# Three conditioning blocks of the second layer computed by VectorE and GpSimd beside the first layer's output product

## What is computed

```python
def adaln(cond, w, b):
    m = jax.nn.silu(cond) @ w + b
    return jnp.split(m[:, None, :], 6, axis=-1)      # shift, scale, gate, and again

for l in range(2):
    mp, ms = adaln(c_ctx[None, :], ada_w[l], ada_b[l]), adaln(c, ada_w[l], ada_b[l])
    hp, hs = modulate(xp, norm_mix[l], mp[0], mp[1]), modulate(xs, norm_mix[l], ms[0], ms[1])
    # layer 0: windowed attention and pooling, then @ a_w_out; layer 1: Fourier mixing, @ f_w_out
    xp, xs = xp + mp[2] * op, xs + ms[2] * os_
    # then a mixture of experts of the same kind, modulated with mp[3..5] and ms[3..5]
```

## Time and profile before

| | us |
|---|---|
| median of 3 runs (772.98 to 773.32) | 773.24 |
| the profiled execution | 773.66 |
| its span, first to last instruction | 771.9 |
| TensorE busy | 754.7 |
| VectorE busy | 373.5 |
| ScalarE busy | 172.9 |
| GpSimd busy | 2.4 |

### The profile page before, as it was taken

How to read it: one execution, slowest core, us unless ns; L and a number is a source line. 1 busy time by engine, 2 the same in 40 slices (tenths; PEclk the granted TensorE clock), 3 DMA queues, 4 the chain that set the end, 5 groups by cost and what they waited for, 6 DMA issues and landing times.

```text
span 771.9 us, 9987 instructions
## 1 busy us (share of the span) xinstructions
PE 754.7 (98%) x3907; PEld 372.4 (48%) x3907; DVE 373.5 (48%) x826; ACT 172.9 (22%) x431; POOL 2.4 (0%) x12
## 2 busy tenths in 40 slices
PE   8999999999999999999998999999999999999997
PEld 3364546445535444434345658445545345444434
DVE  2216174137635345336327996636733454345316
ACT  4111565026301110110115203016211101110111
POOL 0000000000000000000000000000000000000000
PEclk9999999999999999999999999999999999999999
DMA  8979999228999999999999967056699999999994
GB/s 340 427 222 429 428 427 427 110 108 313 349 391 425 427 429 426 428 428 426 422 413 428 425 286 324 3 218 240 250 375 425 428 426 429 425 430 424 424 416 183
DMA packets 32850, 277.04 MB, mean 359 GB/s; under 512 B 7789, under 2 KB 8833, under 8 KB 12833
## 3 DMA queue, kind: packets, MB, share of 16 engines
q1 hardware_dynamic: 32305, 274.96, 86.4%
q10 hardware_dynamic: 432, 1.28, 0.5%
q0 software_dynamic: 64, 0.13, 0.0%
HBM read 274.65 MB, written 1.70 MB: 358 GB/s over the span
## 4 chain that ended last, share of the span: by engine, by line
PE 87%; DMA 4%; DVE 4%; ACT 2%; issue 1%; DVEq 1%; SPq 0%; ACTq 0%
PE bank L2130 28%; PE bank L2155 14%; PE bank L1996 11%; PE bank L2109 5%; PE bank L2161 5%; PE bank L2555 5%; PE bank L2425 4%; PE bank L1924 3%; DMA ring<-in_moe_w 3%; PE bank L2386 3%; DMA ring<-in_ada_w 1%; PE bank L2498 1%; PE bank L2477 1%; PE bank L2141 1%; PE bank L2136 1%
## 5 line engine op out<-in xcount | busy, mean ns | idle before, releaser
L2130 PE MATMUL bank<-ring,Z 128*64 128x512 f32 x1024 | 226.5, 594 | 0.5 <-DMA ring<-in_moe_w 0.5
L2130 PEld LDWEIGHTS bank<-ring,Z 128*64 128x64 f32 x1024 | 72.6, 137 | 137.2 <-issue 135.2
L2155 PE MATMUL bank<-ring,Z 128*64 128x512 f32 (+1 forms) x544 | 113.9, 570 | 0.2 <-DMA ring<-in_moe_w 0.2
L1996 PE MATMUL bank<-ring,T 128*128 128x512 f32 x192 | 83.6, 593 | 0.4 <-issue 0.4
L2155 PEld LDWEIGHTS bank<-ring,Z 128*64 128x64 f32 x544 | 37.9, 137 | 68.2 <-issue 66.1
L1609 DVE TENSOR_TENSOR Z<-Z,bank 128x512 f32<-128x512 f32 x16 | 11.0, 688 | 120.0 <-PE bank L2130 120.0
L1996 PEld LDWEIGHTS bank<-ring,T 128*128 128x128 f32 x192 | 36.0, 190 | 44.5 <-issue 44.5
L2161 PE MATMUL bank<-ys,Cs 128*128 128x512 f32 (+1 forms) x204 | 52.1, 390 | 1.1 <-DVE ys L1626 1.1
L1603 DVE COPY Z<-bank 128x512 f32<-128x512 f32 x24 | 16.6, 692 | 73.7 <-PE bank L2109 73.7
L1639 DVE TENSOR_TENSOR x<-x,bank 128x512 f32<-128x512 f32 x84 | 51.9, 681 | 0.3
L1217 ACT ACTIVATE ys<-wg 128x512 fp32r<-128x512 f32 (+1 forms) x34 | 20.6, 606 | 131.4 <-DVE wg L1621 131.4
(11 more groups left out here) (251 smaller groups left out, 764.3 us busy)
## 6 DMA issues: line engine op xcount, KB each, us to landing
ring<-in_moe_w SPq DMA_DIRECT2D x62, 2048.0 KB, 16.0
ring<-in_moe_w SPq DMA_DIRECT2D x60, 1024.0 KB, 11.0
ring<-in_ada_w SPq DMA_DIRECT2D x23, 2048.0 KB, 19.8
ring<-in_moe_w SPq DMA_DIRECT2D x16, 512.0 KB, 20.2
ring<-in_a_w_out SPq DMA_DIRECT2D x2, 2048.0 KB, 15.9
ring<-in_f_w_in SPq DMA_DIRECT2D x2, 2048.0 KB, 27.0
ring<-in_f_w_out SPq DMA_DIRECT2D x2, 2048.0 KB, 21.0
ring<-in_ada_w SPq DMA_DIRECT2D x2, 1024.0 KB, 8.2
```

The costliest lines, as they stand in the source:

```text
L1996: last = pe.matmul(b[:, :], T[:, k, i * P:(i + 1) * P], w[:, k, :], start=(k == 0), stop=(k == KT - 1))
L2130: last = pe.matmul(out[BLK * u:BLK * (u + 1), :], xT[:, b, k, s0 + BLK * u:s0 + BLK * (u + 1)], w[:, k, :], start=(k == 0), stop=(k == KT ...
L2155: last = pe.matmul(out, aT[:, k, BLK * u:BLK * (u + 1)], down_columns(w2, k, a, e), start=(k == 0), stop=(k == FC - 1), skip_group_check=True)
```

## The change

Blocks 10 to 13 are no longer one joined group of TensorE. Block 10 stays a product of TensorE. Blocks 11 and 12 are weighed by VectorE: 5 steps ahead of the output product of layer 0, then 4, 4 and 3 steps after its first three tiles. Block 13 is weighed by GpSimd, from the time when VectorE has copied the last attention tile: for each slice two products with a condition into `pool_row` and, from the second slice on, one addition of 1024 columns to the sums, with a drain after the products and after the addition. Behind the fifth tile of the output product, TensorE waits for both and adds the three blocks' sums into bank 6 beside block 10 (`summed_rows(0)`, 6 products by `pick`). ScalarE copies the bank, and the transposes and VectorE's finish of the group come after the first norm transposes. The product of block 9 and its transposes come later in the attention. The slots of items 14, 15 and 16 come free when VectorE and GpSimd have read them.

```diff
-JOINED = [range(n, n + 4) for n in (6, 10)]
-SUMMED = range(14, 18)
+JOINED = [range(6, 10)]
+SUMMED = [range(10, 14), range(14, 18)]
+POOL_SUMMED = [13]
+PE_SUMMED = [10]
+DVE_SUMMED = [n for g in SUMMED for n in g if n not in [*POOL_SUMMED, *PE_SUMMED]]
+ROWS_BEHIND = [(0, 1, 1), (1, 0, NT - 1)]
...
-                    return (summed, SUMMED.index(m) + 1) if m in SUMMED else (full, turn[("ada", m)][1])
+                    if m in DVE_SUMMED:
+                        return summed, DVE_SUMMED.index(m) + 1
+                    if m in POOL_SUMMED:
+                        return pool_summed, POOL_SUMMED.index(m) + 1
+                    return full, turn[("ada", m)][1]
...
+            gp.wait_ge(dve_emptied, turn[("oT", NT - 1)][3])
+            for n in POOL_SUMMED:
+                at, j = ada_at(n), n - SUMMED[0][0]
+                gp.wait_ge(arrived[at % NS], 16 * (at // NS + 1))
+                for k in range(KT):
+                    w = ring[:, at % NS, HALF * k:HALF * (k + 1)]
+                    for c in range(2):
+                        by = cond[:, k, COND_AT + c:COND_AT + c + 1]
+                        last = gp.tensor_scalar(ada_sum(n, c) if k == 0 else pool_row[:, c, :], w, by, None, ALU.mult)
+                    if k > 0:
+                        gp.drain()
+                        last = gp.tensor_tensor(ada_sums[0][:, j, :, :], ada_sums[0][:, j, :, :], pool_row, ALU.add)
+                    if k == KT - 1:
+                        last.then_inc(pool_summed, 1)
+                    gp.drain()
...
             def norm_ffn_act(l):
                 s = 2 * l + 1
                 rms(s, 0)
+                if l == 0:
+                    ada_product(SUMMED[0][-1])
                 rms(s, 1)
...
+            ROUNDS = [(4, 4, 3, 0, 0, 0), (4, 2, 0, 0, 0, 0)]
...
-                        if (l, hh) == (1, 0):
-                            weigh((4, 2, 0)[i])
+                        weigh(ROUNDS[l][n])
+                        if (l, hh, i) == (0, 1, 1):
+                            ada_read(SUMMED[0][-1])
...
             attended(2)
+            weigh(5)
             gated_add(0)
...
-            def summed_rows():
-                pe.wait_ge(summed, len(SUMMED))
-                b = begin(("ada", SUMMED[-1]))
+            def summed_rows(l):
+                pe.wait_ge(summed, len([n for g in SUMMED[0:l + 1] for n in g if n in DVE_SUMMED]))
+                pe.wait_ge(pool_summed, len(POOL_SUMMED))
+                b = begin(("ada", SUMMED[1][-1])) if l else banks[JOINED_BANK]
...
-                        if (l, hh, i) == (1, 0, NT - 1):
-                            summed_rows()
+                        if (l, hh, i) in ROWS_BEHIND:
+                            summed_rows(l)
```

More of the change, by code:

```diff
@@ L307, in project @@
                 t.add(("out", l, hh, i), "dve")
-                if (l, hh, i) == (1, 0, NT - 1):
-                    t.add(("ada", SUMMED[-1]), "act")
+                if (l, hh, i) == ROWS_BEHIND[0]:
+                    t.whole(("ada", SUMMED[0][-1]))
+                    t.empty(("ada", SUMMED[0][-1]))
+                    t.banks = list(range(7))
+                if (l, hh, i) == ROWS_BEHIND[1]:
+                    t.add(("ada", SUMMED[1][-1]), "act")
                 if (l, hh, i) == (1, 1, 0):
-                    ada_read(SUMMED[-1])
+                    ada_read(SUMMED[1][-1])
                 if (hh, i) == (1, 1):
                     norm(2 * l + 1, 0)
+                    if l == 0:
+                        ada_read(SUMMED[0][-1])
         norm(2 * l + 1, 1)
@@ L424, in plan @@
     scores(1, 0)
-    ada_product(9)
     values(0, 0)
     scores(1, 1)
-    ada_read(9)
+    t.whole(("ada", 9))
+    values(0, 1)
+    t.empty(("ada", 9))
+    scores(2, 0)
     ada_product(10)
-    values(0, 1)
-    scores(2, 0)
-    ada_product(11)
     values(1, 0)
     scores(2, 1)
-    ada_product(12)
     values(1, 1)
-    ada_product(13)
+    ada_read(9)
     values(2, 0)
-    ada_read(13)
     values(2, 1)
-    t.banks = list(range(7))
     project(0)
@@ L1188, in _ @@
             turned(0, 1)
+            ada_product(9)
             exps(1, 1)
@@ L1412, in low_part @@
                     emptied_inc(last)
-            weighting = [(j, k) for j in range(len(SUMMED)) for k in range(KT)]
+            weighting = [(n, k) for n in DVE_SUMMED for k in range(KT)]
             def weigh(n):
-                for j, k in weighting[0:n]:
-                    at = ada_at(SUMMED[j])
+                for m, k in weighting[0:n]:
+                    at = ada_at(m)
                     if k == 0:
@@ L1425, in weigh @@
                         if k == 0:
[L1426 removed]
+                            last = dve.tensor_scalar(ada_sum(m, c), w, by, None, ALU.mult)
                         else:
[L1428 removed]
+                            last = dve.scalar_tensor_tensor(ada_sum(m, c), w, by, ada_sum(m, c), ALU.mult, ALU.add)
                     if k == KT - 1:
@@ L1971, in normed_cols @@
                 done_by(("norm", s, t, 0), ("norm", s, t, 1))
-            def summed_rows():
-                pe.wait_ge(summed, len(SUMMED))
-                b = begin(("ada", SUMMED[-1]))
+            def summed_rows(l):
+                pe.wait_ge(summed, len([n for g in SUMMED[0:l + 1] for n in g if n in DVE_SUMMED]))
+                pe.wait_ge(pool_summed, len(POOL_SUMMED))
+                b = begin(("ada", SUMMED[1][-1])) if l else banks[JOINED_BANK]
                 for c in range(2):
-                    for j in range(len(SUMMED)):
+                    for j, n in enumerate(SUMMED[l]):
+                        if n in PE_SUMMED:
+                            continue
                         at = PICK_AT - (4 * j + c)
-                        last = pe.matmul(b[32 * j:32 * j + 32, :], pick[:, at:at + 32], ada_sums[:, j, c, :],
-                                         start=(c == 0), stop=(c == 1), skip_group_check=True)
+                        last = pe.matmul(b[32 * j:32 * j + 32, :], pick[:, at:at + 32], ada_sum(n, c),
+                                         start=(l == 1 and c == 0), stop=(c == 1), skip_group_check=True)
                 last.then_inc(full, 1)
```

41 lines of the change are left out of this document (20 added, 21 removed).

## The result

The changed kernel takes **794.15 us** (median of 4, 791.83 to 794.73) against 773.21 (772.98 to 773.32) before: a ratio of 1.0263, 95% interval 1.025 to 1.0276. It is slower, by 20.9 us where 9.9 were forecast. The profiled execution took 793.88 us. The 20 us arose in three places: the wait for the sums, what stands right behind it, and a branch 230 us later. The prediction had only the first.

The account below looks back on a forecast made before the run. TensorE was taken to bound the kernel, busy 754.7 of 771.9 us. Attention -5.5 and output product +2.4 give -3.1; with a 12.9 us wait, 773.7 - 3.1 + 12.9 - 0.4 = 783.1 us, 8-in-10 range 769.4 to 790.

Parts of the forecast that it names:

- Attention, -5.5: Attention of layer 0: three blocks and the transposes leave TensorE, 6.2 us, less 0.7 exposed; between -6.2 and -3.5.
- The fourth rival: Attention bound by its exponentials, giving 3.5 us less, vectors in time: 773.6 us; chance 0.10 together with partial blocking.
- +2.4 in the output product: Output product on TensorE: 6 multiplications with `pick` add 1.85 us and the moved transposes 0.5.
- GpSimd alone, 22.5 us: GpSimd's block during the output product: 16 products and 7 additions, 21.0 us, plus 1.5 us for 15 drains.
- My high bound of 33.8 us: GpSimd's block with each stream in and out paid apart: 16 x 0.95 + 7 x 2.66 us.
- the window of 34.2 us: Output product: time from VectorE's last attention copy at 127.4 us to TensorE's reading of the sums at 161.6.
- Taking turns over the whole block: Output product: VectorE and GpSimd alternate except for three gated products, 47.1 us; TensorE waits 12.9; 783.1 us, chance 0.58.
- The rival "side by side": Output product: VectorE and GpSimd work without delaying TensorE, each fitting the window; 770.2 us, faster, chance 0.32.
- Each late microsecond is paid in full: Behind TensorE's wait for the sums stand the sixth tile, norm transposes and router, so lateness counts one for one.
- VectorE's margin of 7.5 us: Output product: VectorE alone needs 26.7 us, done at about 154, 7.5 us before the sums are wanted.
- everything later shifted by one constant: Sign that the forecast is right: behind the output product all later work moves by the same amount.
- The ring at nothing: Slots freed later delay four loads; costed at nothing while GpSimd ends before about 180 us, later up to 5 us.

Follow-up runs that it names:

- e2: Changed kernel with GpSimd stopped after the first of eight slices of block 13, the rest left out: 775.08 us, ratio 1.0019.
- e3: Changed kernel with VectorE stopped after the first of eight slices of blocks 11 and 12, so GpSimd works nearly alone: 787.82 us, ratio 1.0185.
- e4: Changed kernel with VectorE's multiply-adds of blocks 11 and 12 reading a PSUM bank in place of the running sum: 787.09 us, ratio 1.0176.
- e1: Changed kernel with 18 tiny products (32 x 8, result unread) on TensorE at the start, restoring its later instructions' places: 789.89 us, ratio 1.0201.
- e8: Kernel before the change with 46 tiny products (32 x 8, result unread) at the start, 184 instructions more on TensorE: 778.72 us, ratio 1.0073.
- e10: e3 with 13 unread products of 512 columns ahead of TensorE's wait for the sums and 5 tiny ones at the start: 783.50 us, ratio 1.0133.

## Why the prediction came out as it did

Slower was right, and so was the place of the wait; the size was not, 20.9 us where 9.9 were forecast. Two terms were wrong and cancelled in the wait: GpSimd's block, and the taking of turns over whole instructions. What the number misses by is two terms that the prediction had at nothing, 4.6 us behind the wait and 4.7 us at the branch; 0.5 us of wait and 0.4 of attention come on top.

**Attention, -5.5: right in size.** The output product starts at 127.44 (127.0 forecast), 5.1 us earlier. The fourth rival, that the removed blocks were cover, fell.

**+2.4 in the output product: right.** 2.5 in e2, where nothing waits; the picks take 1.9 us. The wait is reached at 162.0 (161.6 forecast).

**GpSimd alone, 22.5 us: the step that failed,** by a factor of two. It measured 45.3 (e3): the products 26.4, the seven additions 16.4, gaps 2.5. The additions were 2.35 us where I took 1.81; the figure of the Trainium skill (GPSIMD Engine Reference, section Performance versus the Vector engine), an estimated 2.3, agrees with this trace. But the large error is the product: 1.65 us where I took 0.52 from the memset, with 0.95 as the high bound. The memset was the nearest row in engine and size and the wrong one in kind, since it doesn't compute. My high bound of 33.8 us for the block was no bound: it priced the streams and gave the arithmetic nothing. Nor did it fit in the window of 34.2 us, as I wrote: with the 1.5 us of drains it is 35.3. The argument that each engine alone fits the window fell with that.

**Taking turns over the whole block: failed as well.** The engines do hold each other up, but they do not take turns. I let their work add up to 47.1 us, and GpSimd's 47.3 look like a hit. They are not: 45.3 of them are its own. With 45.3 for GpSimd my rule gives 26.7 + 45.3 - 2.1 = 69.9 us and a wait of 35.7; the wait was 13.4. Most of the work overlaps: VectorE loses some 2 us beside each of GpSimd's additions, 0.4 us where an instruction starts just after one of GpSimd's products has, nothing where it starts later in the product, and nothing where it has an operand in PSUM (e4). That makes 44.6 us on VectorE, 26.7 alone (e2 confirms: 155.3), and 2 us on GpSimd. The wait of 13.4 us next to 12.9 forecast is luck: GpSimd's work was too small by half, and what the two cost each other too large. The rival "side by side" would have failed with no interference at all: 11.3 us of wait in e3.

**"Each late microsecond is paid in full": too cheap.** Behind the wait came 4.6 us more than the 2.4 forecast. I let VectorE's margin of 7.5 us be used up and didn't ask what VectorE does next: the norm, which TensorE wants at once, and which a VectorE done at 172.4 delivers at 179.6. 2.5 of the 4.6 us are this wait, and 2.1 the clock: it fell to 1.2 GHz while TensorE stood, and was still there not only for the picked rows (3.64 us instead of 1.9, hidden by the norm) but for all up to 184 us. The square has the two apart: 1.7 to 2.7 us with the norm early and the clock low, 4.1 with the norm late and the clock full at first. The split of the 4.6 is read from rows.

**Nothing for 72 instructions fewer: missed.** 4.7 us at the branch in layer 0 (e1, e8). The prediction had "everything later shifted by one constant"; it shifted by 15.3 and then by 20.

**The ring at nothing: right.** Its condition held, since GpSimd ended at 175.2, before 180. The loads were issued up to 52 us later (item 22 at 172.4, not 120.4). Items 22 and 23 landed at 179.9 and 184.8, before the 190 that was to be the sign, and no product of the mixture waited for a load in this kernel. In e1 and e10 one waits 0.8 and 0.7 us.

The sum as it should have stood: -5.1 + 2.4 + 13.4 + 4.6 + 4.7 = +20.0; the second branch shows 20.0, the span 19.4, the median 20.9.

## What to carry to other kernels

Price an engine's work by a row of the same operation; a memset or a copy says nothing of a multiplication on GpSimd, and a sum of streams is no upper bound. Where a helper shares a memory path with an engine, ask for both: when the helper is done, and what that engine owes the critical path next; here either one alone would have lost the gain. An engine's own time and the time it takes from its neighbour are two prices, and a total that fits says nothing of either. And when an edit changes the number of TensorE's instructions, look at each branch of its program in both traces before explaining the time: in this kernel its place is worth 4.7 us, more than the whole change could have won.

## What the runs showed of the hardware that I had not expected

- GpSimd multiplies a float32 column of 128 rows in 3.0 ns and copies it in 1.13; the addition of two takes 2.3. The product with one input tile is slower than the addition with two.
- A branch over an unused body takes 0.5 to 2.1 us or 6.0 to 6.2 us on TensorE (its first pass, in layer 0), by its place in the program; 184 tiny instructions more act like 72 fewer.
- VectorE's multiply-add from PSUM and SBUF runs at full pace beside GpSimd (5.86 us for eight), that from two SBUF tiles at 9.3 to 11.2. Beside a GpSimd addition it waits for nearly the whole of it (2.83 us for 0.75), beside a product for 0.4 us. Products by a scalar from SBUF are held too (1.37 us for some 0.45).
- Filling a wait of 13 us kept the clock full until the next wait, of 2.40 us, behind which it was low again (0.76 of full over 177 to 184 us): 0.8 us won. Where no second wait followed, 2.7 us were won in the same stretch.
